# Weight pieces of 1024 columns by half of the rows, a first retrieval round done head by head, and two steps moved earlier, in a streaming encoder step

## The reference

```python
def layer(x, ...):
    h = rmsnorm(x, g_mix)
    z = h @ w_in                                   # 1024 x 2048: u, v, xb, gate
    ya, v_rows = gmlp_mix(jax.nn.gelu(z[..., :1024]), g_v, w_s, b_s)
    xc, new_buf = causal_conv(z[..., 1024:1536], conv_buf, conv_w, conv_b)
    yb, h_last = rg_lru(xc, h0, w_a, b_a, w_i, b_i, lam)
    yb = yb * jax.nn.gelu(z[..., 1536:])
    x = x + jnp.concatenate([rmsnorm(ya, g_out_a), rmsnorm(yb, g_out_b)], axis=-1) @ w_out
    return x + peer(rmsnorm(x, g_ffn), w_q, k1, k2, u_tab, v_tab), ...

def peer(...):                                     # per token, 8 heads
    q = (xb @ w_q).reshape(128, 8, 2, 128)
    s1, s2 = scores of q[:, :, 0] and q[:, :, 1] against 128 keys each
    v1, i1 = lax.top_k(s1, 16); v2, i2 = lax.top_k(s2, 16)
    top_s, sel = lax.top_k(v1[..., :, None] + v2[..., None, :], 16)   # over 256 sums
    eidx = (i1 * 128 + i2) at sel                  # 16 experts per head, 128 per token
    act = gelu(dot(u_tab[eidx], xb)); coef = softmax(top_s) * act
    return sum over 128 experts of coef * v_tab[eidx]
```

## Time and profile before

| | before |
|---|---|
| median of three runs | 1807.57 us (1798.82 to 1817.49) |
| the profiled execution | 1806.61 us |
| its span, first to last instruction | 1804.9 us |
| mean granted TensorE clock | 0.905 of 2.4 GHz |
| PE busy | 1455.9 us (81%) |
| DVE busy | 1425.8 us (79%) |
| POOL busy | 806.3 us (45%) |
| ACT busy | 634.0 us (35%) |
| moved by DMA | 675.75 MB, 374 GB/s over the span |

### The profile page before, as it was taken

The page is one execution under the profiler, slowest core; times in us unless marked ns, Lnnn a source line. Parts: engine busy times, 40 slices in busy tenths (PEclk is TensorE's granted clock), DMA queues, the critical chain, the costliest instruction groups (busy, mean ns, idle before and its releaser), DMA issues.

```text
span 1804.9 us, 16904 instructions
## 1 busy us (share of the span) xinstructions
PE 1455.9 (81%) x4706; PEld 790.5 (44%) x4706; DVE 1425.8 (79%) x3039; ACT 634.0 (35%) x1935; POOL 806.3 (45%) x667
## 2 busy tenths in 40 slices
PE   6799796666675652886969988999998788999997
PEld 5485344333342212644735655433334555433332
DVE  1277788999898779689998989996668988766665
ACT  4335633322222221330147776221115666311112
POOL 2023234577776667668734444222223554322220
PEclk9899898888886785988989999999998888999998
DMA  9489999999999999999988989999998999999996
GB/s 355 153 329 409 405 364 403 336 407 397 402 397 407 378 415 384 389 340 391 385 311 321 355 330 371 417 417 417 416 417 347 362 371 365 387 417 417 417 417 257
DMA packets 146478, 675.75 MB, mean 374 GB/s; under 512 B 15216, under 2 KB 15472, under 8 KB 97232
## 3 DMA queue, kind: packets, MB, share of 16 engines
q0 software_dynamic: 92832, 538.39, 75.6%
q1 hardware_dynamic: 50496, 132.68, 19.1%
q10 hardware_dynamic: 3056, 3.61, 0.6%
HBM read 671.61 MB, written 3.01 MB: 374 GB/s over the span
## 4 chain that ended last, share of the span: by engine, by line
PE 32%; DMA 28%; DVE 17%; issue 8%; ACT 8%; POOL 7%; ACTq 0%; DVEq 0%; SPq 0%; POOLq 0%
DMA arena<-experts 19%; PE accY L1497 9%; DMA ring<-experts,idc 8%; PE pb L1482 8%; POOL ring L624 6%; PE pb L1302 4%; DVE ring L924 3%; DVE ring L913 3%; PE pb L1471 3%; ACT arena L1227 2%; PE pb L1311 2%; PE pq L1428 2%; DVE arena L973 2%; DVE arena L975 1%; PE pb L1320 1%
## 5 line engine op out<-in xcount | busy, mean ns | idle before, releaser
L622 POOL DMA_INDIRECT ring<-experts,idc x384 | 467.3, 1217 | 842.0 <-DVE xt L933 374.1
L913 DVE CUSTOM_DVE_ANT_0 ring<-ring,h 128x1024 f32<-128x1024 f32 x384 | 466.0, 1221 | 197.3 <-DMA ring<-experts,idc 196.2
L1497 PE MATMUL accY<-ring,diag 128*128 128x512 f32 x792 | 452.1, 707 | 202.6 <-ACT diag L1213 202.5
L1482 PE MATMUL pb<-arena 128*128 128x512 f32 x1024 | 472.7, 607 | 19.8 <-DMA arena<-experts 13.2
L624 POOL DMA_INDIRECT ring<-experts,idc x256 | 328.7, 1284 | 111.8 <-issue 74.5
L1202 ACT ACTIVATE ge<-zt 128x1 f32<-128x1 f32 x384 | 76.4, 199 | 767.6 <-DVE zt L913 766.1
L1497 PEld LDWEIGHTS accY<-ring,diag 128*128 128x128 f32 x792 | 158.2, 217 | 410.5 <-ACT diag L1213 276.3
L1482 PEld LDWEIGHTS pb<-arena 128*128 128x128 f32 x1024 | 186.1, 191 | 304.8 <-issue 197.3
L933 DVE SCALAR_TENSOR_TENSOR xt<-ring,coef,xt 128x1024 f32<-128x1024 f32 x186 | 238.2, 1281 | 13.1 <-ACT coef L1206 13.0
L924 DVE CUSTOM_DVE_ANT_0 ring<-ring,arena 128x1024 f32<-128x1024 f32 x128 | 153.3, 1221 | 8.6 <-DMA ring<-experts,idc 7.5
L1227 ACT ACTIVATE arena<-arena,qT 128x64 f32<-128x64 f32 x512 | 129.1, 334 | 83.4 <-DVE arena L975 83.4
(11 more groups left out here) (178 smaller groups left out, 1080.1 us busy)
## 6 DMA issues: line engine op xcount, KB each, us to landing
arena<-experts SPq DMA_DIRECT2D x128, 512.0 KB, 15.1
arena<-w_q SPq DMA_DIRECT2D x12, 2048.0 KB, 19.7
arena<-w_in SPq DMA_DIRECT2D x11, 2048.0 KB, 21.8
ring<-experts,idc POOLq DMA_INDIRECT x640, 9.2
arena<-w_out SPq DMA_DIRECT2D x4, 2048.0 KB, 20.7
ring<-w_out SPq DMA_DIRECT2D x2, 2048.0 KB, 20.0
xt<-x_all SPq DMA_DIRECT2D x5, 512.0 KB, 13.5
y_all<-xt ACTq DMA_DIRECT2D x5, 512.0 KB, 3.5
```

The lines of the kernel that those rows point to most:

```text
L622: nc.gpsimd.indirect_dma_start(ring[:, at // 2], None, experts, index).then_inc(gat[at], 16)
L913: V.tensor_tensor_reduce(out=half(g), in0=half(g), in1=h2[:], scale=1.0, scalar=0.0, op0=ALU.mult, op1=ALU.add, accum_out=zt[:, s % 8:s % ...
L1482: ins = T.matmul(pb[:, 2 * j + k], cm[:, i, j * P:(j + 1) * P], vring[:, n % VRING, k * 512:(k + 1) * 512], start=i == 0, stop=i == BLOCKS ...
L1497: ins = T.matmul(accY[:, j], diag[:, (n - 1) % DIAGS], ring[:, place, D + j * 512:D + (j + 1) * 512], start=first, stop=final)
```

## The change

Five edits, all in one kernel.

1. A piece of `w_in` or `w_out` now holds 1024 columns of 512 rows instead of 512 columns of 1024 rows. It is still 2 MB, but a row of it is 4 KB instead of 2 KB. REC0 and REC1 are the upper and the lower half of the rows of the xb and gate columns; MIX0 and MIX1 the same for u and v; OUT0 and OUT1 the halves of `w_out`. A product that sums over all rows therefore reads two pieces, and waits for both at its first matmul. The pieces of `w_q` stay as they were.
2. A place is free again when both column groups of its pieces are done (semaphore cols_done, which counts xb, gate, v, u of each front), so the planner puts the pieces elsewhere.
3. The first round of tile 0 is done head by head. PE makes the queries of head 0, scores them in a bank of their own and only then goes on; DVE finds head 0's sixteen experts from start to end (`one_head(0)`), then one step of front 1, then head 1. POOL's first sixteen gathers wait for head 0 alone.
4. The expert numbers of tiles 1 and 2 are written and transposed twenty dots before the end of tile 2 (item `ids`), into a place of their own (`stage`, where `xc` was); only the coefficients stay in `prep`, which now stands behind tile 3's first dot, and `adopt(3)` no longer waits for the transposes.
5. At the end take 4 and norm 4 come before flush 1.

```diff
-LAST = [0, 3, 1, 2, 4]
+LAST = [0, 3, 4, 1, 2]
...
-XB, GATE, VV, UU, OUT0, OUT1, WQ0 = 0, 1, 2, 3, 4, 5, 6
+REC0, REC1, MIX0, MIX1, OUT0, OUT1, WQ0 = 0, 1, 2, 3, 4, 5, 6
-PIECE_START = {4: XB, 6: GATE, 10: VV, 13: UU, 20: OUT0, 24: OUT1}
-PIECE_END = {5: XB, 7: GATE, 11: VV, 14: UU, 23: OUT0, 25: OUT1}
+PIECE_START = {4: (REC0, REC1), 10: (MIX0, MIX1), 20: (OUT0, OUT1)}
+PIECE_END = {7: (REC0, REC1), 14: (MIX0, MIX1), 25: (OUT0, OUT1)}
+XB, GATE, VV, UU = (REC0, 0), (REC0, PW), (MIX0, PW), (MIX0, 0)
...
-        if x < 4:
-            order.append(("I", 1, x))
-            order.append(("Iv", 1, x))
+        if x in (0, 1, 4, 5):
+            order.append(("I", 1, (0, 1, 4, 5).index(x)))
+            order.append(("Iv", 1, (0, 1, 4, 5).index(x)))
...
-    put.append((b + 0.01, ("prep",)))
+    put.append((b - 12.01, ("ids",)))
     put.append((b + 0.02, ("adopt", 3)))
+    put.append((b + 0.2, ("prep",)))
...
                     if j < OUT0:
-                        sp.wait_ge(piece_done, 4 * old + j + 1)
+                        sp.wait_ge(cols_done, 4 * old + (2 if j < MIX0 else 4))
                     elif j < WQ0:
-                        sp.wait_ge(out_done, OUT_BASE[old] + (j - OUT0 + 1) * len(FRONTS[old]))
+                        sp.wait_ge(out_done, OUT_BASE[old + 1])
...
+            def one_head(u):
+
+                hs = slice(u, u + 1)
+                v.wait_ge(sc_done if u else sc_first, 1)
+                best_keys(u, psc if u else accY[:, 0])
+                sums(hs)
+                next_eight(hs)
+                if u:
+                    negate_best(0, 0)
+                else:
+                    st.after()
+                differences(hs)
+                numbers(hs)
+                st.gives(V.scalar_tensor_tensor(out=idc[:, 0, u * TOPK:(u + 1) * TOPK], in0=e12[:, u, 0],
+                                                scalar=float(P), in1=e12[:, u, 1], op0=ALU.mult, op1=ALU.add),
+                         idx_ready, u + 1)
...
             def by_channel(f, k, bank, half):
 
                 w = width(f)
-                wt = piece(f, k)
+                first, at = k
+                wts = [piece(f, first), piece(f, first + 1)]
...
+                    if n == 0 and x == 0:
+                        a.wait_ge(q_first, 1)
+                        A.activation(qT[:, 0:256], accY[:, 1, 0:256], ACT.Copy).then_inc(qT_first, 1)
```

More of the change, by code:

```diff
@@ L167, in weave @@
             put.append((b + 5.02, ("norm", 3)))
[L168 to L172, removed]
+    put.append((b + 2.0, ("take", 4)))
+    put.append((b + 2.1, ("norm", 4)))
+    put.append((b + 2.2, ("flush", 1)))
+    put.append((b + 2.3, ("norm", 1)))
+    put.append((b + 2.4, ("norm", 2)))
     put.sort(key=lambda e: e[0])
@@ L218, in piece_edges @@
             _, f, p = item
[L219 to L222, removed]
+            for k in PIECE_START.get(p, ()):
+                first.append((f, k))
+            for k in PIECE_END.get(p, ()):
+                done[f, k] = len(done) + 1
         if item[0] == "II" and item[1] < 2:
@@ L853, in next_sums @@
-            def next_sums(f, r):
-                top_eight(1, [left[:, 0], left[:, 1]], [best[:, 0], best[:, 1]], [sel[:, 0], sel[:, 1]], None,
-                          [st.last, st.last])
+                    cand[:, hs, TOPK:].rearrange("p h (a b) -> p h a b", b=8),
+                    vals[:, hs, 0, 1:].unsqueeze(3).to_broadcast([P, n, TOPK - 1, 8]),
+                    vals[:, hs, 1, 0:8].unsqueeze(2).to_broadcast([P, n, TOPK - 1, 8]), ALU.add))
+                us = range(hs.start, hs.stop)
@@ L856, in next_sums, with numbers, negate_best @@
+            def numbers(hs):
+                ks = slice(2 * TOPK * hs.start, 2 * TOPK * hs.stop)
+                st.after()
+                st.step(V.tensor_reduce(e12[:, hs].rearrange("p h e k -> p (h e k)"), eqm[:, ks], AX_X, ALU.min,
+                                        apply_absolute_value=True))
+                st.after()
+            def negate_best(f, r):
                 guard = st.gives(V.tensor_scalar(nmax[:], best[:, :, 0], -1.0, None, ALU.mult), best_done,
@@ L1307, in by_token @@
             def by_token(f, k, j):
-                wt = piece(f, k)
+                first, at = k
+                wts = [piece(f, first), piece(f, first + 1)]
                 b = BANK[f]["v" if k == VV else "u"]
                 for c in range(DC):
-                    ins = T.matmul(pb[:, b + j], hT[:, c, j * P:(j + 1) * P], wt[:, c], start=c == 0,
-                                   stop=c == DC - 1)
+                    ins = T.matmul(pb[:, b + j], hT[:, c, j * P:(j + 1) * P], wts[c // HC][:, c % HC, at:at + PW],
+                                   start=c == 0, stop=c == DC - 1)
@@ L1427, in queries, with score @@
                     for c in range(DC):
[L1428 to L1429 removed]
+                        out = accY[:, 1, q * w:(q + 1) * w] if n == 0 and first else pq[:, q * w:(q + 1) * w]
+                        ins = T.matmul(out, wt[:, c, o:o + P], h2T[:, c, 0:w], start=c == 0, stop=c == DC - 1)
                 if not first:
                     ins.then_inc(q_done, 1)
+                elif n == 0:
+                    ins.then_inc(q_first, 1)
+            def score(f, q, u, out):
+                w = width(f)
+                for e in range(2):
+                    o = (2 * u + e) * P if f == 0 else e * w + u * P
+                    ins = T.matmul(out[:, (2 * u + e) * P:(2 * u + e + 1) * P], q[:, o:o + P], keys[:, e], start=True,
+                                   stop=True)
+                return ins
             def retrieve(f, x):
[L1434 removed]
                 for r in range(ROUNDS[f]):
                     n = ROUND_BASE[f] + r
+                    if n == 0 and x == 1:
+                        t.wait_ge(qT_first, 1)
+                        t.wait_ge(rows_in, 48)
+                        score(f, qT, 0, accY[:, 0]).then_inc(sc_first, 1)
                     if f < 2 and x in (5 * r, 5 * r + 1):
```

202 lines of the change are left out of this document (118 added, 84 removed).

## The result

The changed kernel takes 1852.99 us (median of four, 1844.60 to 1859.41), the kernel before 1811.68 beside it: a ratio of 1.0244, 95% interval 1.0208 to 1.0279. It is slower, as forecast, but by more than 40 where the forecast said 25, and it lies above the range (1797 to 1850).

A forecast was written before the change was run, and what follows sets the result against it. It took DMA to bound where big tables stream, but PE or DVE in the stages changed. Terms 13.0 + 6.3 - 2.0 + 10.7 - 1.6 - 0.7 - 0.6 = +25.1 on 1806.6 gave 1832; range 1797 to 1850.

The forecast's parts named there:

- start of front 0's products: Front 0: the first matmul waits for the second piece, landing at 23.1, so products start 6.5 later.
- first gather: First round of tile 0: head 0's numbers come early, so POOL's first gather goes out at about 104.6 for 106.7.
- front 1's xb, start included: Front 1: xb waits for REC1, taken to land in 13 beside gathers; +13.0 (8 to 18).
- front 1's v: Front 1: MIX1 is issued only when gate ends, so v waits 6.3 (1.3 to 11.3).
- rest of front 1, to the first dot of tile 1: Front 1 until 205: PE's gaps make good some of the waits; -2 (0 to -2).
- packets, to the start of front 2: Twelve remaining pieces: longer rows save at most 0.53 each; -1.6 granted (0 to -6.4).
- front 2: Front 2: v starts 13 later waiting for MIX1, DVE makes up about half of its idle 5.2; +10.7 (4 to 17).
- early numbers: Before tile 3's norm: DVE's wait of 1.72 for PE goes, a wait for ACT's gelu replaces it; -0.7 (0 to -3).
- end: After the last dense sum: two norms follow instead of three, but the sum starts late; -0.6 (0 to -2.6).
- first rival: Whole kernel: DMA is the bound, landed gathers absorb PE and DVE waits; 1799, at best 1789; chance 0.22.
- The second, landings of 8 to 9 beside gathers: Fronts 1 and 2: waits exist, but longer-row pieces land in 8 to 9 even beside gathers; 1815; chance 0.22.
- The third: Tile 0's first round: head 0's numbers not early, first gather at 106.7 + 6.5; adds at most 2; chance inside the forecast's.

The follow-up runs named there:

- d0: Changed kernel with the new half-row pieces in front 0 alone, fronts 1 and 2 loading by columns as before: 1811.47, ratio 1.0007.
- a2: Changed kernel with the old weight pieces, all other edits kept: 1806.02, ratio 0.9977 to the kernel before.
- a3: Kernel before with the head by head first round alone: 1810.33, ratio 1.0002.
- g1: Changed kernel run once more, nothing altered, in a second set of runs: 1853.52, ratio 1.0261 to the kernel before.
- a4: Kernel before with the early key numbers and the early last norm alone: 1808.41, ratio 0.9999.
- a1: Kernel before with the new weight pieces alone: 1838.71, ratio 1.0148.
- b1: Changed kernel with all gathers held back until front 1's REC1 has landed: 1846.34, ratio 1.0221 to the kernel before.
- d2: Changed kernel with the new half-row pieces in front 2 alone: 1821.36, ratio 1.0079 to the kernel before.
- f4: Changed kernel with all gathers held until the event on which REC1 is issued, so they go behind it: 1842.00, ratio 1.0206 to the kernel before.
- e1: Changed kernel with each product waiting for the second row half only at a group's fifth matmul: 1851.33, ratio 1.0216 to the kernel before.
- c_in: Changed kernel with `w_out` again in pieces of 512 columns, only `w_in` by half rows: 1847.51, ratio 1.0233 to the kernel before.
- c_out: Changed kernel with the old `w_in` pieces, only `w_out` by half rows: 1813.60, ratio 1.0038 to the kernel before.
- b2: Changed kernel with each half-row piece loaded by two DMAs of 512 columns, so 2 KB rows: 1859.41, ratio 1.0288 to the kernel before.
- f3: Changed kernel with all but three gathers held back until front 1's REC1 has landed: 1846.86, ratio 1.0210 to the kernel before.
- d1: Changed kernel with the new half-row pieces in front 1 alone: 1831.94, ratio 1.0129 to the kernel before.

## Why the prediction was wrong

Right in direction and in most of its places, wrong in size. The terms against the profiled execution of the kernel after (milestones of its trace less those of before):

| term | forecast | measured |
|---|---|---|
| start of front 0's products | +6.5 | +5.95 (22.60 for 16.65); 0.3% at the end by d0 over a2, with intervals that overlap |
| first gather | 104.6 | 104.60; to the tenth by luck, since without the late start (a3) it went at 99.23 where 98 was expected, and the start came 0.55 earlier |
| front 1's xb, start included | +13.0 | +19.85 (128.22 for 108.37) |
| front 1's v | +6.3 | +6.4: a wait of 4.16, and 2.1 since xb's first half ran 9.15 for 7.07; the agreement is luck, g1 has +3.4 with a wait of 1.63 |
| rest of front 1, to the first dot of tile 1 | -2.0 | +6.0: 1.1 by the queries behind v, 4.9 later |
| packets, to the start of front 2 | -1.6 | -7.6 for the whole stretch, not told apart: a4, which changes nothing there, has -6.1 |
| front 2 | +10.7 | +14.9: v starts 11.3 later, runs 16.68 for 13.90, and 0.8 come behind |
| `w_q` pieces behind front 2 | none | +4.1 (4.4 to 4.6 in a1, b1, d2 and g1) |
| early numbers | -0.7 | tile 3's norm comes 3.3 less late than the dot before it, but by 1400 it is +1; a4 shows no effect |
| untouched stretch, 1400 to 1540 | none | +5.8, not there in g1 |
| end | -0.6 | -2.1 (last block +50.5, last norm +48.3) |

Two of its sums are a little off, and neither changes what follows: front 2's 13 less half of 5.2 is 10.4, not 10.7, and the first rival's best is 1792.5 by its own figures, not 1789.

The step that failed is this one: "Six gathers stand in the queue at that moment, but the piece's rows are twice as long; I take the middle, 13." REC1 took 20.05, more than the upper bound of 18, and that is 7 of the missing 22. The bound was the row of a piece in the kernel before that met gathers already thinned out by POOL's waits (issued at 122.01, 126.09, 128.12 and then 138.29); here the piece met six within 6.3, three ahead of it and three close behind. The prediction had both numbers, first gather 104.6 and REC1's issue 108.3, and did not ask what the order between them is worth. a1 and b1 show 7.9 and 7.8 with no gather in the queues, f4 11.4 with all six behind. The head by head order was credited with an earlier start; in the runs it is the cause of the longest wait.

The second failure is what was left out behind the waits. Two places come free together and late, so loads leave SP in pairs: the `w_q` piece behind MIX1 took 33.2, OUT0, OUT1 and the next `w_q` piece leave between 223.79 and 227.36, and behind front 2 two `w_q` pieces are issued 0.4 apart where they were 14.4 apart. This was written down for SP's queue and given no price; with the -2 that PE was to give back it makes +6.0 for -2.0 and +4.1 for nothing, 12 together. In this execution little of the +6.0 comes from the first of these pieces: it landed at 200.45, just as PE came to it, and the work behind v stands only 1.1 later than v's own start. In g1, a1, b1, f4 and e1 PE did wait for it (3.9 to 6.8). The other 4.9 come between 250 and 275. OUT1 and the `w_q` piece behind it (issued at 227.36) land there beside gathers, and DVE waits for gathers, 5.95 in all, where the same stretch of the kernel before has 0.53. Two of these waits, and that piece:

```profile
260.77 1.22 DVE L976 CUSTOM_DVE_ANT_0 ring<-ring,h 128x1024 f32<-128x1024 f32 x1 [1.87 <-DMA ring<-experts,idc]
273.76 1.23 DVE L976 CUSTOM_DVE_ANT_0 ring<-ring,h 128x1024 f32<-128x1024 f32 x1 [2.01 <-DMA ring<-experts,idc]
...
arena<-w_q SPq DMA_DIRECT2D x1, 2048.0 KB, 48.0
```

Every run with the new pieces in front 1 loses 3.8 to 5.9 from the 29th to the 37th dot of tile 0, c_in with its `w_out` in columns among them; no other run loses more than 0.4 there, and c_out, with the new `w_out` pieces at the old times, loses nothing. So it is the late issue, not the shape of the `w_out` pieces.

A third thing had no term: behind its waits PE ran slower. xb's first half took 9.15 for 7.07, v's in front 1 9.90 for 7.03, and v in front 2 16.68 for 13.90, 7.7 together (last section).

Front 2 was the right mechanism with a size a little off: MIX1 landed in 12.7 (14.5 forecast), v waited 11.14, DVE 21.52 at its reciprocal (near 20 forecast). But DVE made none of it good, and v itself ran 2.8 longer. The dips of DMA came at 128 and 795, not at 125 and 775: the gathers and the pieces kept it full for as long as PE waited, and the holes came when POOL had no place left (its 27.52 before 139.36 and 18.67 before 806.03).

The first rival, DMA as the bound, fell, but not by the test that the prediction set for it. PE's wait of 13.34 stayed under the 15 that six gathers were to keep DMA busy, and DMA did stay busy (398 GB/s). It then moved 1 GB/s for 12, since the mix that frees a place stands behind xb, and xb had yet to run. The wait and the product behind it count together. The second, landings of 8 to 9 beside gathers, fell with 20.0 and 12.7, though its rule stands (below); only MIX1 of front 1 comes near it, with 10.9 here and 8.3 in g1. The third fell: the first gather was early.

## What to carry to other kernels

Before a load is given a second partner to wait for, list what else is in the DMA queues at its issue, with bytes and row lengths, and price the landing from that; a landing measured in another company is no bound. An edit that starts a stream earlier is not free where another engine sits waiting for a load issued a moment later: with the first gather 3.4 ahead of REC1 it landed in 20, with the order turned round in 11.4. Where a stream feeds from places that the waiting engine frees, count the wait and the work behind it: DMA stood still after the wait, not in it. And when a wait is shortened, ask which transfer is late next, since pieces whose places come free together land one behind the other.

## What the runs showed of the hardware

Where both queues have work they move equal numbers of packets, and a packet in these traces is one row (apart from some packets of 4 bytes). In the changed kernel POOL's queue (q0) and SP's (q1) moved, from 117 to 121 (8 KB gather rows, 4 KB piece rows) and from 780 to 785 (4 KB and 4 KB): packets, MB, share.

```profile
q0 software_dynamic: 149, 1.08, 64.0%
q1 hardware_dynamic: 149, 0.61, 37.5%
...
q1 hardware_dynamic: 271, 1.07, 53.5%
q0 software_dynamic: 269, 0.98, 49.1%
```

And in b2 from 785 to 790, with 2 KB piece rows beside 4 KB gather rows:

```profile
q0 software_dynamic: 370, 1.33, 65.6%
q1 hardware_dynamic: 368, 0.73, 37.6%
```

The counts are equal to within 1%, so a piece's share of the bytes is near its row over the sum of both rows: a third, a half, a third (measured 0.36, 0.52 and 0.35). At 417 GB/s a piece of 2.10 MB then takes about 15, 10 and 15. That is an estimate; measured from issue to landing were 20.0, 12.7 and 18.5 (in b2 v's start less MIX1's issue at 774.18). REC1's excess is its start: its first packet came 3.73 after its issue, and its 512 rows then took 15.4, near the estimate. From 108.1 to 111.7 only the gathers moved, and from 111.7 to 113 both did:

```profile
q0 software_dynamic: 185, 1.38, 99.1%
...
q0 software_dynamic: 49, 0.31, 61.8%
q1 hardware_dynamic: 34, 0.14, 31.1%
```

In f4, where the gathers came second, it is the other way round. From 107.4 (their first issue) to 111.6 only the piece's queue moved:

```profile
q1 hardware_dynamic: 317, 1.30, 96.1%
```

With empty queues a piece's first packet came 1.0 after its issue (a1, b1, f4) and a gather's 1.7 (changed kernel, b1); behind the other queue's work 3.5 to 3.7 (g1, f3, d1, d2) and 4.2 (f4). So in this stage whoever came second lost 2.5 to 2.7 more before the equal turns began; why, stays open. In front 1 row length hardly counted (14.46 for 13.34), and the likely reason, argued and not tested, is volume: the six gathers and the piece, 8.4 MB, take 20 at 417 GB/s in any order, and the piece was among the last to end.

The Trainium skill (DMA: Bandwidth & Descriptors, section on queues, rings and completion order) says that an engine goes round its queues by packets. The equal counts above agree; how many rows one turn holds they don't show. The prediction named the rule and worked it out wrongly: a 4 KB row beside 8 KB rows gets a third of the bytes, and no landing of 8 follows from it.

PE's clock: after standing idle for 13.34 PE ran xb's first half in 9.15 for 7.07, and the window from 125 to 150 has a mean granted clock of 0.85 of 2.4 GHz where the earlier trace rows has 1.00, so part of it ran at the lower level of 1.2. A wait of 13.34 cost 15.4. The same holds behind two of the other waits: after 4.16 v's first half took 9.90 for 7.03 in front 1, with a mean granted clock of 0.71, and after 11.14 v took 16.68 for 13.90 in front 2, with 0.84; the same stretches of the kernel before have 1.00. The prediction had no term for this.
